# Two transformer blocks on one core: the stick attention's steps moved to other units of the last projection, and two small steps moved in the first

## The reference, cut to what matters

```python
proj = jnp.einsum('bsd,dc->bsc', h, w_in[layer])       # 2048 -> 4*2048 + 8
qkv = proj[..., :3 * MIX_WIDTH].reshape(bsz, seq, 3, N_MIXERS, N_HEADS_PER_MIXER, HEAD_DIM_2)
o_a = dilated_attention(...)          # mixer 0
o_b = stick_breaking_attention(q[1], k[1], v[1])        # mixer 1, "stick"
o_c = moba_attention(...)             # mixer 2
o_d = forgetting_attention(...)       # mixer 3
y = y * jax.nn.silu(gate)
x = x + jnp.einsum('bsc,cd->bsd', y, w_out[layer])
```

```python
z = jnp.einsum('bhqd,bhkd->bhqk', qi, k) * SCALE
log_1mb = jnp.where(causal, jax.nn.log_sigmoid(-z), 0.0)
after = lax.cumsum(log_1mb, axis=3, reverse=True) - log_1mb
log_a = jnp.where(causal, jax.nn.log_sigmoid(z) + after, NEG)
return jnp.einsum('bhqk,bhkd->bhqd', jnp.exp(log_a), v)
```

## Time and profile before

| | |
|---|---|
| median of 3 runs | 2938.99 us (2938.47 to 2941.37) |
| profiled execution, its own time | 2938.93 us |
| its span in the profile | 2937.1 us |
| TensorE busy | 2929.6 us |
| VectorE busy | 2040.9 us |
| ScalarE busy | 1465.2 us |
| GpSimd busy | 292.9 us |
| granted TensorE clock, mean | 1.00 |

### The profile page before, as it was taken

One profiled execution on the slowest core, in us unless ns is written; L12 is line 12 of the kernel. 1 busy time (PEld: TensorE's weight loads), 2 busy tenths in 40 slices (PEclk: granted clock), 3 DMA queues, 4 the chain that ended last, 5 costly groups with the idle time before them and its releaser, 6 DMA issues.

```text
span 2937.1 us, 37967 instructions
## 1 busy us (share of the span) xinstructions
PE 2929.6 (100%) x13590; PEld 2409.4 (82%) x13590; DVE 2040.9 (69%) x2730; ACT 1465.2 (50%) x1832; POOL 292.9 (10%) x269
## 2 busy tenths in 40 slices
PE   9999999999999999999999999999999999999999
PEld 7888888888888878888888888888878888888887
DVE  6676766766557868667667665667787677778764
ACT  6654444444445554554444444445556545555653
POOL 1110000000005431100000000002500000430000
PEclk9999999999999999999999999999999999999999
DMA  8766666666666546666666666566555556655555
GB/s 303 235 187 194 192 192 194 193 192 194 194 194 189 163 137 195 193 201 192 193 193 193 192 193 194 186 200 196 162 167 165 164 181 186 187 153 174 161 165 172
DMA packets 281617, 551.52 MB, mean 188 GB/s; under 512 B 17056, under 2 KB 19376, under 8 KB 281104
## 3 DMA queue, kind: packets, MB, share of 16 engines
q1 hardware_dynamic: 276592, 531.19, 59.7%
q0 software_dynamic: 4752, 18.35, 1.8%
q10 hardware_dynamic: 144, 0.26, 0.0%
HBM read 542.92 MB, written 6.82 MB: 187 GB/s over the span
## 4 chain that ended last, share of the span: by engine, by line
PE 98%; DMA 1%; DVE 1%; ACT 1%; issue 0%; SPq 0%; ACTq 0%
PE ps L522 24%; PE ps L1074 22%; PE ps L578 16%; PE ps L530 12%; PE ps L1081 11%; PE ps L549 8%; PE ps L1227 1%; PE ps L1294 1%; DMA w_raw<-xattn_w_kv 1%; PE ps L1327 1%; PE ps L1202 0%; PE ps L1355 0%; PE ps L883 0%; ACT w_hi L418 0%; DVE w_lo L425 0%; PE ps L824 0%
## 5 line engine op out<-in xcount | busy, mean ns | idle before, releaser
L425 DVE TENSOR_TENSOR w_lo<-w_raw,w_hi 128x1024 fp32r<-128x1024 f32 x1008 | 1251.5, 1246 | 813.6 <-ACT w_hi L418 803.5
L418 ACT ACTIVATE w_hi<-w_raw 128x1024 fp32r<-128x1024 f32 x1007 | 1064.6, 1059 | 1329.2 <-PE ps L530 541.2
L1074 PE MATMUL ps<-w_hi,actT_hi 128*128 128x512 f32 x1408 | 547.9, 389 | 0.0
L1074 PE MATMUL ps<-w_hi,actT_lo 128*128 128x512 f32 x1408 | 547.7, 389 | 0.0
L578 PE MATMUL ps<-w_hi,actT_hi 128*128 128x512 f32 x960 | 385.9, 402 | 0.0
L1081 PE MATMUL ps<-w_lo,actT_hi 128*128 128x512 f32 x1408 | 376.3, 389 | 0.0
L578 PE MATMUL ps<-w_hi,actT_lo 128*128 128x512 f32 x960 | 374.7, 390 | 0.0
L522 PE MATMUL ps<-w_hi,hidT_hi 128*128 128x512 f32 x864 | 318.9, 390 | 0.3 <-DVE hidT_hi L1384 0.3
L1074 PEld LDWEIGHTS ps<-w_hi,actT_lo 128*128 128x128 f32 x1408 | 264.4, 188 | 54.9
L1081 PEld LDWEIGHTS ps<-w_lo,actT_hi 128*128 128x128 f32 x1408 | 264.3, 188 | 54.9
L1074 PEld LDWEIGHTS ps<-w_hi,actT_hi 128*128 128x128 f32 x1408 | 264.2, 188 | 54.7
(11 more groups left out here) (325 smaller groups left out, 3171.8 us busy)
## 6 DMA issues: line engine op xcount, KB each, us to landing
w_raw<-ffn_w_in SPq DMA_DIRECT2D x352, 512.0 KB, 4.3
w_raw<-w_in SPq DMA_DIRECT2D x256, 512.0 KB, 3.7
w_raw<-ffn_w_out SPq DMA_DIRECT2D x176, 512.0 KB, 4.6
w_raw<-w_out SPq DMA_DIRECT2D x64, 512.0 KB, 4.0
w_raw<-attn_w_in SPq DMA_DIRECT2D x48, 512.0 KB, 3.7
w_raw<-attn_w_out SPq DMA_DIRECT2D x32, 512.0 KB, 3.8
w_raw<-xattn_w_kv SPq DMA_DIRECT2D x31, 512.0 KB, 7.3
w_raw<-xattn_w_q SPq DMA_DIRECT2D x16, 512.0 KB, 3.7
```

Source lines behind the costliest of these rows:

```text
L418: nc.scalar.activation(w_hi[:, v % NS], w_raw[:, v % NS], ACT.Copy).then_inc(w_hi_done, 1)
L425: nc.vector.tensor_tensor(w_lo[:, v % NS], w_raw[:, v % NS], w_hi[:, v % NS].bitcast(F32), ALU.subtract).then_inc(w_lo_done, 1)
L1074: nc.tensor.matmul(ps[:, 2 * b + tb], lhs[:, k, tb * P:(tb + 1) * P], w_hi[:, s, kk * CB:(kk + 1) * CB], start=(k == 0 and part == 0), sto ...
```

## The change

In the mixer layers: stick scores 0 and 1 go from unit 45 to 42, ahead of mixer `m == 2`'s last values at that unit (TensorE's stick steps now stand ahead of its mixer steps in every unit), and all steps of pieces 0 and 1 go with them, three units earlier, in all three lists. Scores 2 and 3 go from 56 to 53, the sums 2 and 3 from 62 and 64 to 60 and 62, and values 2 and 3 from 67 to 72. Pieces get other PSUM banks (`Z_BANK`, `OUT_BANK`), with waits to suit. VectorE's normalising of mixer 3's queries and keys is spread over slightly other units and its square root on ScalarE goes from 60 to 57. In kv0: ScalarE's sines from step 7 to 8, VectorE's cosines from 8 to 9, and the scaling of `band` from behind split 12 to ahead of it.

```diff
+        Z_BANK = (4, 2, 4, 6)
+        OUT_BANK = (2, 3, 6, 7)
...
         def pe_stick_z(pe, l, q):
...
-            if q == 0:
-                pe.wait_ge(qt_copied, stages[f"s{l}"][1]["n"] + 1)
+            pe.wait_ge(qt_copied, stages[f"s{l}"][g]["n"] + 1)
+            pe.wait_ge(pt_copied, stages[f"m{l}"][7]["n"] + 1)
+            if q == 3:
+                pe.wait_ge(o_done, stages[f"m{l}"][7]["group"] + 1)
+            b = Z_BANK[q]
...
+            if q == 0:
+                pe.wait_ge(st_neg, 4 * l + 2)
...
-            steps = {45: [(pe_stick_z, 0), (pe_stick_z, 1)], 51: [(pe_stick_r, 0)], 53: [(pe_stick_r, 1)],
-                     56: [(pe_stick_v, 0), (pe_stick_v, 1), (pe_stick_z, 2), (pe_stick_z, 3)],
-                     62: [(pe_stick_r, 2)], 64: [(pe_stick_r, 3)], 67: [(pe_stick_v, 2), (pe_stick_v, 3)]}
-            if pos_ == 45:
-                pe.wait_ge(o_done, stages[f"m{l}"][7]["group"] + 1)
-            if pos_ == 56:
+            steps = {42: [(pe_stick_z, 0), (pe_stick_z, 1)], 48: [(pe_stick_r, 0)], 50: [(pe_stick_r, 1)],
+                     53: [(pe_stick_v, 0), (pe_stick_v, 1), (pe_stick_z, 2), (pe_stick_z, 3)],
+                     60: [(pe_stick_r, 2)], 62: [(pe_stick_r, 3)], 72: [(pe_stick_v, 2), (pe_stick_v, 3)]}
+            if pos_ == 53:
                 pe.wait_ge(row_free[1], in_rest(l, 9))
...
-                steps = {50: [(low_part, 0)], 51: [(low_part, 1)], 61: [(low_part, 2)], 62: [(low_part, 3)]}
+                steps = {47: [(low_part, 0)], 48: [(low_part, 1)], 59: [(low_part, 2)], 60: [(low_part, 3)]}
             else:
-                steps = {45: [(scores, 0)], 46: [(scores, 1)], 48: [(softplus, 0)], 49: [(softplus, 1)],
-                         51: [(weights, 0)], 53: [(weights, 1)], 56: [(scores, 2)],
-                         57: [(scores, 3), (out, 0), (out, 1)], 59: [(softplus, 2)], 60: [(softplus, 3)],
-                         62: [(weights, 2)], 64: [(weights, 3)], 67: [(out, 2), (out, 3)]}
+                steps = {42: [(scores, 0)], 43: [(scores, 1)], 45: [(softplus, 0)], 46: [(softplus, 1)],
+                         48: [(weights, 0)], 50: [(weights, 1)], 53: [(scores, 2)],
+                         54: [(scores, 3), (out, 0), (out, 1)], 57: [(softplus, 2)], 58: [(softplus, 3)],
+                         60: [(weights, 2)], 62: [(weights, 3)], 72: [(out, 2), (out, 3)]}
...
-            steps = {46: [(power, 0)], 47: [(power, 1), (logs, 0)], 48: [(logs, 1)], 49: [(high_part, 0)],
-                     50: [(high_part, 1)], 52: [(weights, 0)], 54: [(weights, 1)],
-                     57: [(power, 2)], 58: [(power, 3), (logs, 2)], 59: [(logs, 3)], 60: [(high_part, 2)],
-                     61: [(high_part, 3)], 63: [(weights, 2)], 65: [(weights, 3)]}
+            steps = {43: [(power, 0)], 44: [(power, 1), (logs, 0)], 45: [(logs, 1)], 46: [(high_part, 0)],
+                     47: [(high_part, 1)], 49: [(weights, 0)], 51: [(weights, 1)],
+                     54: [(power, 2)], 55: [(power, 3)], 56: [(logs, 2), (logs, 3)], 58: [(high_part, 2)],
+                     59: [(high_part, 3)], 61: [(weights, 2)], 63: [(weights, 3)]}
...
-            if pos_ == SCORED[8] - 2:
+            if pos_ == SCORED[8] + 8:
                 pe.wait_ge(y_st, 4 * l + 4)
...
                 def in_rest_pe(pos_):
+                    pe_stick(pe, l, pos_)
                     pe_mixers(pe, l, pos_)
-                    pe_stick(pe, l, pos_)
...
-                if t == 7:
+                if t == 8:
                     act_angles(act)
...
-                    if pos_ == 60:
+                    if pos_ == 57:
                         act_heads(act, l, 2)
...
-                if t == 8:
+                if t == 9:
                     dve_cosines(dve)
-            split_turns(dve, dve_split, "kv0", mid=in_kv0)
+
+            def before_kv0(i, b, j):
+                if 8 * b + j == 12:
+                    band_scales()
+            split_turns(dve, dve_split, "kv0", mid=in_kv0, begin=before_kv0)
...
-                             52: (2, 0), 54: (2, 1), 55: (2, 2), 58: (2, 3), 61: (2, 4), 63: (2, 5), 65: (2, 6),
-                             66: (2, 7), 67: (2, 8)}
+                             51: (2, 0), 52: (2, 1), 55: (2, 2), 56: (2, 3), 61: (2, 4), 63: (2, 5), 64: (2, 6),
+                             65: (2, 7), 66: (2, 8)}
```

More of the change, by code:

```diff
@@ L1607, in pe_stick_z @@
             buf = stages[f"s{l}"][g]["buf"]
-            if q == 0:
-                pe.wait_ge(qt_copied, stages[f"s{l}"][1]["n"] + 1)
+            pe.wait_ge(qt_copied, stages[f"s{l}"][g]["n"] + 1)
[3 more added lines that the diff above has]
+            b = Z_BANK[q]
             for hh in range(2):
                 h = p + hh
-                nc.tensor.matmul(ps[:, 4 + p + hh, 0:256], head_ops(buf, 1, h, 0, P), head_ops(buf, 0, h, 0, SEQ),
+                nc.tensor.matmul(ps[:, b + hh, 0:256], head_ops(buf, 1, h, 0, P), head_ops(buf, 0, h, 0, SEQ),
                                  start=True, stop=True)
-                mm = nc.tensor.matmul(ps[:, 4 + p + hh, 256:384], head_ops(buf, 1, h, P, SEQ),
+                mm = nc.tensor.matmul(ps[:, b + hh, 256:384], head_ops(buf, 1, h, P, SEQ),
                                       head_ops(buf, 0, h, P, SEQ), start=True, stop=True)
@@ L1639, in pe_stick_v @@
                 v = [proj(2, 1)[:, kb, c0 + hh * 64:c0 + (hh + 1) * 64] for kb in range(2)]
-                o = ps[64 * hh:64 * hh + 64, 2 + p // 2]
+                o = ps[64 * hh:64 * hh + 64, OUT_BANK[q]]
                 nc.tensor.matmul(o[:, 0:SEQ], v[0], Z[:, hh * SEQ:(hh + 1) * SEQ], start=True, stop=False)
@@ L1662, in scores @@
                     m = strictT[:, lo:lo + n].rearrange("p (o n) -> p o n", o=1).broadcast_to([P, 2, n])
-                    mark(nc.vector.scalar_tensor_tensor(out=heads_of(Z, 2 * lo, n), in0=ps[:, 4 + p:6 + p, lo:lo + n],
+                    mark(nc.vector.scalar_tensor_tensor(out=heads_of(Z, 2 * lo, n), in0=ps[:, Z_BANK[q]:Z_BANK[q] + 2, lo:lo + n],
                                                         scalar=0.125, in1=m, op0=ALU.mult, op1=ALU.add))
@@ L1687, in out @@
                 dve.wait_ge(st_o, 4 * l + q + 1)
-                nc.vector.tensor_copy(out_home(1)[:, q], ps[:, 2 + p // 2, 0:SEQ]).then_inc(y_st, 1)
+                nc.vector.tensor_copy(out_home(1)[:, q], ps[:, OUT_BANK[q], 0:SEQ]).then_inc(y_st, 1)
             if before:
-                steps = {50: [(low_part, 0)], 51: [(low_part, 1)], 61: [(low_part, 2)], 62: [(low_part, 3)]}
+                steps = {47: [(low_part, 0)], 48: [(low_part, 1)], 59: [(low_part, 2)], 60: [(low_part, 3)]}
             else:
-                steps = {45: [(scores, 0)], 46: [(scores, 1)], 48: [(softplus, 0)], 49: [(softplus, 1)],
-                         51: [(weights, 0)], 53: [(weights, 1)], 56: [(scores, 2)],
-                         57: [(scores, 3), (out, 0), (out, 1)], 59: [(softplus, 2)], 60: [(softplus, 3)],
-                         62: [(weights, 2)], 64: [(weights, 3)], 67: [(out, 2), (out, 3)]}
+                steps = {42: [(scores, 0)], 43: [(scores, 1)], 45: [(softplus, 0)], 46: [(softplus, 1)],
+                         48: [(weights, 0)], 50: [(weights, 1)], 53: [(scores, 2)],
+                         54: [(scores, 3), (out, 0), (out, 1)], 57: [(softplus, 2)], 58: [(softplus, 3)],
+                         60: [(weights, 2)], 62: [(weights, 3)], 72: [(out, 2), (out, 3)]}
             for step, q in steps.get(pos_, []):
@@ L2540, in _ @@
                 .then_inc(fing_done, 1)
-            norms = {t: step for t, (_, step) in zip((11, 12), dve_norm_steps(dve, "mix0"))}
+            (_, band_variance), (_, band_scales) = dve_norm_steps(dve, "mix0")
             def in_kv0(i, b, j):
@@ L2553, in in_kv0 @@
                     dve_mem_pair(dve, t // 2 + 2)
-                if t in norms:
-                    norms[t]()
+                if t == 11:
+                    band_variance()
                 if t == 7:
                     dve_angles(dve)
-                if t == 8:
+                if t == 9:
                     dve_cosines(dve)
-            split_turns(dve, dve_split, "kv0", mid=in_kv0)
+            def before_kv0(i, b, j):
+                if 8 * b + j == 12:
+                    band_scales()
+            split_turns(dve, dve_split, "kv0", mid=in_kv0, begin=before_kv0)
             dve_turn(dve, "mix0", "mix0", hidT_hi, hidT_lo, YT, part=(0, 4))
```

## The result

The changed kernel takes 2950.01 us (median of 6 runs, 2948.75 to 2952.24) against 2939.6 us for the kernel before (median of 6, 2938.47 to 2941.37): ratio 1.0037, 95% interval [1.0027, 1.0047]. It is slower by 10.4 us, 0.35% by the medians. The profiled execution took 2950.14 us, with a span of 2948.3 us and a mean granted clock of 0.998.

What follows compares the result with a forecast made beforehand. TensorE's matmuls plus its waits were taken to bound the kernel. 2938.93 us, less 1.35 for the front, plus 7.26 for the two layers' waits net of merges, gave 2944.84 (2944.8) us; range 2942.3 to 2949.0.

Steps and rivals of the forecast that it cites:

- The bound: Whole kernel: TensorE, busy for all but 7.5 us of the span, sets the time by its matmuls and its waits.
- Part 3: First stick half, both mixer layers: unit 48 waits for ScalarE's row copy, 3.83 us later per layer; 7.26 for both, net.
- Part 1: Angles and band in kv0: the waits at unit 12 (0.75 us) and the banded turn (0.60) go, saving 1.35 us.
- rival 3: Start of the run: the front gives nothing because memory paces supplies there; 2946.2 us, chance 0.06.
- Part 2: Stick scores at 42 and values at 72: each excursion less saves TensorE 0.20 us, two less in each mixer layer.
- Part 4: Second stick half, both mixer layers: moved scores, sums and values stay covered, with no wait at 60, 72 or 80; nothing.
- Rival 2: Mixer layers: no wait appears, as all three engines' steps shift together; 2936.8 us, chance 0.14.
- rival 1: Wait before unit 48: TensorE's clock falls to half, costing at most 2.3 us per layer, 1.9 taken; 2948.6 us, chance 0.23.
- a fall behind the copy: Sign at the row copy of unit 47, both mixer layers: if the granted clock falls behind it, the prediction is wrong.

Runs made afterwards that it cites:

- r6_quarters: The changed kernel with the second stick job's four quarters on VectorE at units 44, 46, 47, 49 instead of 38 to 41: 2942.02 us, ratio 1.0008.
- r3_chain_back: The changed kernel with the logarithms and later steps of pieces 0 and 1, and the second half up to the sums, at their old units: 2937.91 us, ratio 0.9994.
- r2_fill: The changed kernel with 16 more matmuls, results unread, on TensorE at the end of unit 47 in both layers: 2946.13 us, ratio 1.0022.
- r4_high_behind: The changed kernel with ScalarE's two high parts one unit later (47 and 48), behind the row copy: 2946.16 us, ratio 1.0022.
- r8_pause_long: The kernel before with one added TensorE wait ahead of unit 48 in both layers, for VectorE's split 47: 2946.98 us, ratio 1.0028.
- r5_stick_only: The changed kernel with the kv0 part undone: 2951.87 us, ratio 1.0043 against the kernel before.
- r1_front: The kernel before with only the kv0 change (sines and cosines a step later, band scaled ahead of split 12): 2938.63 us, ratio 0.9997.

## Why the prediction was wrong

**What held.** The bound (TensorE's own list plus its waits) and the place of the wait were right. Part 3 held term by term: the start of unit 48 was worked out at 3.83 us later and came 3.86 us later once the 0.36 of this execution's lead is taken off (2206.29 + 0.36 - 2202.79). Its cause held against undoing each half: without the backlog 1.2 us are left (r6_quarters), with the chain behind the copy nothing (r3_chain_back). Part 1 was put at 1.35 and measured 1.7: unit 12 gave its 0.75, the matmuls behind it 0.13 more, and at the banded turn entry costs nothing at all here. But three of the six profiled executions with the new front lose most of this again for a late load, as rival 3 had it. Part 2 was put at 0.20 a merge and measured 0.21 at 42 and 0.22 at 72. Part 4 held: the trace has no wait at 60, 72 or 80. Rival 2 (no wait) is out.

**The step that failed** is the choice between the forecast and rival 1. The sum of the forecast took TensorE's clock to stay full through a pause of 4.0 us and gave that 0.53, against 0.23 for the fall. In all six runs of the changed kernel the mean clock was 0.998, and its fall is what lies between 2944.8 and 2950 (r2_fill, with the same wait and a full clock, is 3.9 us faster): 2944.84 + 2.80 + 1.43 = 2949.07, and with the later start and the better front (+1.37 - 0.37) 2950.07, where the profiled execution has 2950.14. The prediction had named a fall behind the copy as a sign that it is wrong. The argument for the lower chance was that one pause at the end of the run proves little. It was the only evidence in the trace, and it pointed to a fall: idleness of 3.4 us was followed by it, and the new pause was longer. The runs since have a mean clock under 1.00 with pauses of 2.6 us in every run and of 3.0 in three of seven, and 1.00 with pauses of 1.7 or 1.2.

**A term that was mis-sized** is rival 1's own price: at most 2.3 us a layer, from the 4.56 us that the first matmuls took, and 1.9 taken, for which no row is given. That those first matmuls ran at the low level is not shown either: the windows there read a clock of 1.00. The low level lasted from 2205.6 to 2212.4 in the first layer, 6.8 us and so longer than those 4.56, and cost 2.80; in the second 1.43. With a top end of 2 x 2.8 the range would have reached past 2950, and the result of 2950.01 would have been inside it. The Trainium skill ("TensorE: Matmul & The Clock Gate", Part 1), which the prediction set beside this rival, said that inactivity sends the clock back to half; the trace after agrees, with 0.50 granted from 2206 to 2212.

**What stays open** is why a pause of 2.6 us always brought the fall in r4_high_behind and one of 3.0 only sometimes in r8_pause_long. The length of the pause alone doesn't decide it. The traces give a hint: in the three profiled executions with falls in both layers (after, r4_high_behind, r5_stick_only) the second fall comes 488.1 us behind the end of the first low stretch every time, although TensorE had then been idle for 3.7, 2.0 and 3.0 us. That points to the moment and not only the length of the pause, but no run here varied the one without the other.

## What to carry to other kernels

On an engine with one ordered list, a step that is moved earlier is only as early as the engine is free: find the moved step's real start from the backlog in the trace, and then look for the bottleneck's own supplies that now stand behind it in the same list (here ScalarE's row copy behind a high part that waits for VectorE). And where the bottleneck is TensorE, price a wait of the length that brought a fall here, 2.6 us and more, with the clock's fall in the sum and not as a side case: here 1.4 to 2.8 us on top of 4.0. If the wait can't be removed, matmuls to no purpose in it can buy that part back, as r2_fill did.

## What the runs showed of the hardware that was not expected

- With idle stretches of 2.6 us the mean granted clock was under 1.00 in all ten runs of one kernel, with 3.0 us in three of seven runs of another; with 1.2 and 1.7 us it was 1.00 in all twenty. The falls that were profiled came after 2.0 to 3.7 us of idleness.
- The low level lasted 6.8 us in one layer and 3.4 in the other, after pauses of the same 4.0 us in the same execution.
- Sixteen useless matmuls in each of the two waits saved 3.9 us together.
- Unit 4, up to which all kernels have the same instructions, starts up to 2.5 us apart in the ten profiled executions; the 33 runs of the kernel before that were taken beside r1_front span 2.9 us.
